# Shift outputs and expert biases moved by DMA instead of TensorE transposes, an early sigmoid table, and a split reciprocal, in a hybrid decoder layer

## The reference, cut to what matters

```python
h = rms_norm(x, norm1) * (1 + sc1) + sh1             # modulation rows from silu(c) @ w_mod
q, k, v, p_rw, g_a, g_b = split(h @ w_in)            # p_rw has RW_COLS = 1792 columns
o_a = sliding_window_attention(q, k, v, cache)       # 8 query heads, 2 key heads
o_b, new_wkv = rwkv7_mix(p_rw, state_shift, state_wkv, ...)
new_shift = p_rw[:, -1]                              # output: last row of p_rw, per sequence
x = x + gt1 * ((sigmoid(g_a)*(o_a@w_pa) + sigmoid(g_b)*(o_b@w_pb)) @ w_o)
h2 = rms_norm(x, norm2) * (1 + sc2) + sh2
# mixture of experts, 32 experts, top 4:
u = h2 @ w1[e] + b1[e]                               # 2048 columns: gate half, linear half
y = (min(u_g,7) * sigmoid(1.702*u_g) * (clip(u_l,-7,7) + 1)) @ w2[e] + b2[e]
```

## Time and profile before

| what | value |
|---|---|
| median of 3 runs | 1269.61 us (1265.81 to 1270.17) |
| profiled execution, its own time | 1269.29 us |
| its span in the profile | 1267.5 us |
| mean granted TensorE clock | 0.992 of full |
| HBM read | 463.91 MB |
| PE, DVE, ACT, POOL busy | 1199.1, 489.7, 266.5, 54.3 us |

### The profile page before, as it was taken

One profiled execution on the slowest core, in us unless ns is written; L12 is line 12 of the kernel. 1 busy time (PEld: TensorE's weight loads), 2 busy tenths in 40 slices (PEclk: granted clock), 3 DMA queues, 4 the chain that ended last, 5 costly groups with the idle time before them and its releaser, 6 DMA issues.

```text
span 1267.5 us, 20297 instructions
## 1 busy us (share of the span) xinstructions
PE 1199.1 (95%) x8057; PEld 576.9 (46%) x8057; DVE 489.7 (39%) x1067; ACT 266.5 (21%) x495; POOL 54.3 (4%) x69
## 2 busy tenths in 40 slices
PE   7999999999999999999999999999999999999998
PEld 5887777788743333333333333333333333333333
DVE  3155756555433334433333333333333333333433
ACT  2013651220321112211112112111111122121110
POOL 0010624000000000000000000000000000000000
PEclk9999999999999999999999999999999999999999
DMA  9976331367699999999999999999999999999996
GB/s 369 381 260 250 110 110 70 102 225 304 248 429 423 415 430 431 430 430 431 432 432 431 432 431 431 431 432 432 431 431 431 431 431 431 432 432 431 430 430 271
DMA packets 57906, 467.22 MB, mean 369 GB/s; under 512 B 5245, under 2 KB 8577, under 8 KB 32618
## 3 DMA queue, kind: packets, MB, share of 16 engines
q1 hardware_dynamic: 55098, 460.55, 86.9%
q0 software_dynamic: 1664, 5.20, 1.5%
q10 hardware_dynamic: 1088, 0.66, 0.2%
HBM read 463.91 MB, written 5.09 MB: 370 GB/s over the span
## 4 chain that ended last, share of the span: by engine, by line
PE 67%; DMA 27%; ACT 2%; DVE 2%; issue 1%; SPq 0%; DVEq 0%
DMA ring<-in_w 27%; PE ps L1557 21%; PE ps L1582 12%; PE ps L972 5%; PE ps L1483 3%; PE ps L962 3%; PE ps L1506 3%; PE ps L1431 2%; PE ps L1399 2%; PE ps L1568 2%; PE ps L980 1%; PE ps L1490 1%; ACT PH L843 1%; PE ps L941 1%; PE ps L917 1%
## 5 line engine op out<-in xcount | busy, mean ns | idle before, releaser
L1557 PE MATMUL ps<-ring,PH 128*64 128x512 f32 x1472 | 327.5, 594 | 23.8 <-DMA ring<-in_w 23.7
L2231 DVE TENSOR_TENSOR SQ<-ps,SQ 128x512 f32<-128x512 f32 x124 | 77.0, 683 | 411.9 <-PE ps L1506 411.8
L1557 PEld LDWEIGHTS ps<-ring,PH 128*64 128x64 f32 x1472 | 103.6, 137 | 239.6 <-issue 188.8
L1582 PE MATMUL ps<-ring,PH 128*64 128x512 f32 x736 | 163.0, 595 | 0.0
L838 ACT COPY PH<-ps 128x512 f32<-128x512 f32 x62 | 33.3, 589 | 576.6 <-PE ps L1557 576.6
L1557 PE MATMUL ps<-arena,PH 128*64 128x512 f32 x504 | 112.2, 594 | 7.5 <-DMA arena<-in_w 7.5
L1582 PEld LDWEIGHTS ps<-ring,PH 128*64 128x64 f32 x736 | 50.8, 137 | 95.8 <-issue 95.8
L1557 PEld LDWEIGHTS ps<-arena,PH 128*64 128x64 f32 x504 | 35.3, 137 | 82.5 <-issue 65.6
L972 PE MATMUL ps<-PH,ring 128*128 128x264 f32 x304 | 69.3, 388 | 0.2 <-issue 0.2
L2224 DVE TENSOR_TENSOR PH<-ps,XR 128x512 f32<-128x512 f32 x31 | 21.4, 692 | 108.4 <-PE ps L1582 108.4
L972 PEld LDWEIGHTS ps<-PH,ring 128*128 128x128 f32 x304 | 57.3, 190 | 10.7 <-issue 1.1
(11 more groups left out here) (485 smaller groups left out, 1173.8 us busy)
## 6 DMA issues: line engine op xcount, KB each, us to landing
ring<-in_w SPq DMA_DIRECT2D x143, 2048.0 KB, 31.5
arena<-in_w SPq DMA_DIRECT2D x46, 2048.0 KB, 31.6
ring<-in_w_mod SPq DMA_DIRECT2D x12, 2048.0 KB, 14.5
ring<-in_w_in SPq DMA_DIRECT2D x8, 2048.0 KB, 12.1
ring<-in_w_o SPq DMA_DIRECT2D x2, 2048.0 KB, 10.7
ring<-in_w_in SPq DMA_DIRECT2D x2, 1024.0 KB, 17.3
ring<-in_w_pa SPq DMA_DIRECT2D x1, 2048.0 KB, 8.1
ring<-in_w_pb SPq DMA_DIRECT2D x1, 2048.0 KB, 9.0
```

Source lines behind the costliest of these rows:

```text
L1557: last = mm(ps[64 * lin:64 * lin + 64, 2 + hh, :], XG[:, k % 4, k // 4, :], slot_row(slot, c, k % 2, lin * FE + hh * 512), start=(k == 0), ...
L1582: last = mm(ps[64 * hh:64 * hh + 64, 4, :], AC[:, f, :], slot_row(slot, c, f % 4, hh * 512), start=(f == 0), stop=(f == NF - 1))
L2231: v.tensor_tensor(acc, ps[:, banks[p // 2][p % 2], :], acc, ALU.add).then_inc(sem["comb_used"], 1)
```

## The change

There are four edits.

1. Shift outputs. The 14 PE transposes and four ACT copies go. POOL copies the nine columns of the 14 chunks into `SHC` (the first 126 floats of `b1T`'s space), and SP, right behind win 6, issues nine DMAs that write `SHC` out element by element: 128 partitions x 14 chunks, each element 4 bytes long in memory order.
2. Expert biases. The load of `b1r`, four PE transposes and a DVE copy go. Behind win 8 SP waits until the nine shift DMAs are done, and loads `b1` straight into `b1T` with features on partitions; `b1T` has its last two dimensions exchanged, so that a piece of 16 bytes is contiguous on both sides.
3. ACT: a one-element sigmoid stands ahead of `mod_rows(8)`, so that the sigmoid table is loaded there.
4. DVE: the reciprocal of the key norms is cut in two halves, the second behind the scans.

```diff
-        b1T = sb("b1T", [P, 4, NE * 4])
+        b1T = sb("b1T", [P, NE * 4, 4])
+        SHC = view(b1T[:, :, :].rearrange("p a b -> p (a b)"), 0, 14, 1 + NS)
@@ SP, the stream
                 if g == AFTER_RWKV[0]:
                     sp.wait_ge(sem["carry_evac"], 5)
-                    sp.wait_ge(sem["sh_out"], 32)
                 if (kind, j) == ("win", 1):
-                    sp.dma_start(b1r, io["b1"].rearrange("(r a) f -> r (a f)", a=4)).then_inc(sem["ld_setup"], 16)
+                if (kind, j) == ("win", 6):
+                    sp.wait_ge(sem["sh_copied"], 1)
+                    for b in range(1 + NS):
+                        row = io["shift_sample"][b - 1:b, :] if b else io["shift_prompt"]
+                        sp.dma_start(row.rearrange("o (c p) -> p c o", p=P), SHC[:, :, b:b + 1],
+                                     allow_slow_non_contiguous=True).then_inc(sem["sh_out"], 16)
+                if (kind, j) == ("win", 8):
+                    sp.wait_ge(sem["sh_out"], 16 + 16 * NS)
+                    sp.dma_start(b1T[:, :, :], io["b1"].rearrange("(r x) y -> r (x y)", x=4).rearrange("r (p f) -> p r f", f=4)).then_inc(sem["ld_b1"], 16)
@@ POOL
-            pool.wait_ge(sem["sh_evac"], 4)
-            pool.dma_start(io["shift_prompt"], ssr[0:1, :]).then_inc(sem["sh_out"], 16)
-            pool.dma_start(io["shift_sample"], ssr[1:9, :]).then_inc(sem["sh_out"], 16)
+            pool.wait_ge(sem["a_evac"], a_end("win4"))
+            pool.tensor_copy(SHC[:, :, :], PTv[:, CR:NCH, NP - 1:T]).then_inc(sem["sh_copied"], 1)
@@ ACT
+            act.activation(warm, epsc[0:1, 0:1], ACT.Sigmoid)
             mod_rows(8)
-            for i in range(4):
-                act.wait_ge(sem["sh_t"], i + 1)
-                w = min(512, RW - 512 * i)
-                act.copy(ssr[0:9, 512 * i:512 * i + w], ps[0:9, 6 + i % 2, 0:w]).then_inc(sem["sh_evac"], 1)
@@ PE
-            for i in range(4):
-                last = tr(ps[:, 7, i * P:i * P + P], b1r[:, i::4], ID)
@@
-            for i in range(4):
-                if i >= 2:
-                    pe.wait_ge(sem["sh_evac"], i - 1)
-                for c in range(4 * i, min(4 * i + 4, 14)):
-                    last = tr(ps[0:9, 6 + i % 2, (c % 4) * P:(c % 4) * P + P], PTv[:, CR + c, NP - 1:T], ID)
-                last.then_inc(sem["sh_t"], 1)
@@ DVE
-            v.tensor_copy(b1T[:, :, :], ps[:, 7, :].rearrange("p (f r) -> p f r", f=4)).then_inc(sem["setup_ready"], 1)
-            chain(v.reciprocal(Rn, Rn))
+            chain(v.reciprocal(Rn[:, 0:2, :], Rn[:, 0:2, :]))
...
             done(v.tensor_tensor(eM, CS, LD[:, :, 0:NP], ALU.subtract), "cs_ready", 2)
+            chain(v.reciprocal(Rn[:, 2:4, :], Rn[:, 2:4, :]))
             chain(v.scalar_tensor_tensor(out=NK, in0=NK, scalar=-1.0, in1=Rn, op0=ALU.mult, op1=ALU.mult))
@@ DVE, before the first expert
+            dve.wait_ge(sem["ld_b1"], 16)
```

More of the change, by code:

```diff
@@ L203, in build @@
         OA = view(PT, 0, 4, T)
-        prow, b1r, ext = view(SG, 2048, P), view(SG, 2176, 512), view(SG, 2688, 384)
+        prow, ext = view(SG, 2048, P), view(SG, 2688, 384)
         crow, csig = view(BM, 0, D), view(BM, 1024, D)
@@ L503, in _ @@
             pool.wait_ge(sem["kmod_ready"], 1)
+            pool.wait_ge(sem["sh_copied"], 1)
             pool.memset(Qz, 0.0).then_inc(sem["pool_part"], 1)
@@ L508, in _ @@
             pool.wait_ge(sem["decays"], 4)
-            pool.wait_ge(sem["sh_t"], 4)
             def by_chunk(x):
@@ L561, in _ @@
             pool.wait_ge(sem["ob_ready"], 1)
-            pool.wait_ge(sem["sh_out"], 32)
+            pool.wait_ge(sem["sh_out"], 16 + 16 * NS)
             pool.wait_ge(sem["st_s"], 32)
@@ L677, in _ @@
             gates(0)
-            act.wait_ge(sem["sh_t"], 4)
+            act.wait_ge(sem["sh_copied"], 1)
             for hp in range(4):
@@ L1011, in _ @@
             pe.wait_ge(sem["ld_cst"], 16)
-            pe.wait_ge(sem["ld_setup"], 48)
-            for i in range(4):
-                last = tr(ps[:, 7, i * P:i * P + P], b1r[:, i::4], ID)
+            pe.wait_ge(sem["ld_setup"], 32)
             for i in range(14):
@@ L1051, in _ @@
             for kv, (t0, nt) in enumerate(TILES[1:]):
-                pe.wait_ge(sem["sh_evac"], 3 + kv)
                 mm(ps[:, 6 + kv, 0:T], II[64 * kv:64 * kv + 64, :], PTv[64 * kv:64 * kv + 64, CK, :], start=True, stop=True)
@@ L1803, in _ @@
             done(last, "setup_ready", 2)
-            dve.wait_ge(sem["ld_setup"], 48)
+            dve.wait_ge(sem["ld_setup"], 32)
             v.tensor_copy(tabx[0:NE, :].rearrange("p (b h) -> p b h", h=HQ), tab[:, :].unsqueeze(1).broadcast_to([NE, NS, HQ])).then_inc(sem["tab_ready"], 1)
             dve.wait_ge(sem["setup_t"], 6)
-            v.tensor_copy(b1T[:, :, :], ps[:, 7, :].rearrange("p (f r) -> p f r", f=4)).then_inc(sem["setup_ready"], 1)
-            chain(v.tensor_copy(SS[:, :, :], ps[:, 5, 0:112].rearrange("p (a b) -> p a b", b=NS)))
+            done(v.tensor_copy(SS[:, :, :], ps[:, 5, 0:112].rearrange("p (a b) -> p a b", b=NS)), "setup_ready", 3)
             v.tensor_copy(brow[:, 0:KEYS], ps[0:NS * HQ, 5, 256:256 + KEYS]).then_inc(sem["brow_ready"], 1)
@@ L1991, in bank @@
                 return ps[:, i, :].rearrange("p (a b) -> p a b", b=CH)
-            dve.wait_ge(sem["sh_out"], 32)
             for n in range(2):
@@ L2241, in hidden @@
                 dve.wait_ge(sem["ut_done"], 2 * i + hh + 1)
-                chain(v.tensor_tensor(UG, u[:, 0], b1T[:, :, column(hh)].broadcast_to([P, 4, C]), ALU.add))
+                chain(v.tensor_tensor(UG, u[:, 0], b1T[:, column(hh), :].rearrange("p r f -> p f r").broadcast_to([P, 4, C]), ALU.add))
                 v.tensor_scalar(UG, UG, 7.0, None, ALU.min).then_inc(sem["ug_ready"], 1)
-                chain(v.tensor_tensor(UL, u[:, 1], b1T[:, :, column(2 + hh)].broadcast_to([P, 4, C]), ALU.add))
+                chain(v.tensor_tensor(UL, u[:, 1], b1T[:, column(2 + hh), :].rearrange("p r f -> p f r").broadcast_to([P, 4, C]), ALU.add))
                 chain(v.tensor_scalar(UL, UL, 7.0, -7.0, ALU.min, ALU.max))
```

## The result

The changed kernel takes 1316.38 us (median of 4, 1314.76 to 1318.56) against 1268.54 us (1265.81 to 1270.17): a ratio of 1.0377, 95% interval 1.0359 to 1.0396. It is slower by 47.8 us, in the direction of rival A and far beyond the range. Its profiled execution took 1315.11 us with a span of 1313.3, which is 45.8 more than before's. Two executions of one later kernel, e8, fell in a slower state of the chip, and ratios leave such executions out.

The account below looks back on a forecast made before the run. The chain of waits before 340 us was taken to set when the DMA-bound expert part starts. Only DVE's 0.9 us gain counted, all else hidden: 1269.6 - 0.9 = 1268.7 us, range 1264 to 1275.

Parts of the forecast that it names:

- rival A: Shift writes ahead of modulation 9: small pieces land late above 31 ns each; at 49.6 ns PE stands 18 us, 1287; chance 0.13.
- The bound: Whole kernel: a microsecond on the chain of waits before 340 us moves the end by one; in the expert loop, nothing.
- PE's path: PE around 120 us: with transposes removed, decay products start at 121.2 instead of 124.27, 3.1 us earlier.
- the cover of the table load: ACT near 118 us: the sigmoid table load of 1.28 us is hidden by modulation 8.
- DVE's side: DVE after the decays: second half reciprocal 3.4 us, normalised keys start at 132.3 instead of 133.19, 0.9 us gained.
- The first probabilities are there at 144.7, PE waits: First group's softmax: DVE and ACT deliver at 144.7; PE, ready at about 142.7, waits 2 us for them.
- rival B: Attention loop: PE's new wait lowers the clock, filler and transposes slow; 1272; chance 0.20.
- the 0.9 us: Gain from normalised keys starting earlier on DVE, the only gain counted in the forecast sum.
- POOL's copy: POOL before the shift writes: 126 elements a partition, done before win 6 is issued at 119.51, costs nothing.
- The price of a piece: DMA cost of one small piece: between 6.6 and 24.8 ns on an engine, taken as 10 ns.
- the 10 us for the shift writes: Nine shift writes behind win 6: 1008 pieces an engine at 10 ns, ending before modulation 9 is delayed, nothing paid.
- Hidden too: Bias load behind win 8: goes in at 197, ends by 222, before pa is issued at 244.22; costs nothing.

Follow-up runs that it names:

- e8: e7 with the reciprocal of the key norms whole again, ahead of the scans; 1271.12 us against 1268.95, ratio 1.0003.
- e9: Kernel before with only the early one-element sigmoid and the reciprocal cut in halves; 1269.4 us against 1268.95, ratio 0.9997.
- e1: Changed kernel with shift rows written in 1,152 pieces of 56 bytes in place of 16,128 of 4; 1272.85 us against 1269.29, ratio 1.0033.
- e2: Kernel of only SP's DMAs, each pattern alone, without the layer; 4-byte writes as in the change 58 ns a piece, reads of that shape 14.
- e5: Changed kernel with shift columns turned by one PE transpose and written in 126 pieces of 512 bytes; 1273.64 us against 1269.29, ratio 1.0028.
- e7: e5 with the bias load moved from behind win 8 to behind win 6; 1267.24 us against 1268.95, ratio 0.9984.
- e4: Changed kernel with the 4-byte shift writes moved behind win 8 and the bias load behind wo 1; 1308.58 us against 1269.29, ratio 1.0313.
- e13: e7 with four filler steps moved ahead of the second scores and POOL's query memset started earlier; 1267.14 us against 1268.88, ratio 0.9979.

## Why the prediction was wrong, by its own steps

- **The bound, PE's path and the cover of the table load: right.** The large delay ahead of 340 us came out at the end one for one (45.3 us at the first expert's load, 45.8 at the end of the span); for a delay of 1.2 us the rule did not hold in e9, where it was gone by pa. The table load is hidden, the products start at 121.34 (121.2 forecast) at a clock of 1.00.
- **DVE's side: right in its steps.** Second half of the reciprocal 3.45 us (3.4), keys at 132.56, and 132.09 in e1 (132.3). PE's wait for DVE was 3.4 us where 2 were forecast, and it came ahead of the second scores, for the copy of the queries, not behind the filler.
- **"The first probabilities are there at 144.7, PE waits": the first half right, the second wrong, because rival B came true as well.** They were there at 144.97. But the filler behind PE's wait took 6.2 to 6.5 us where 3.83 is the full clock's time, and the first transposes came at 146.5 to 147.1, behind before's 145.79. The granted clock of 140 to 150 us was 0.69 in the changed kernel, 0.74 in e1, 1.00 before. That ate the 0.9 us and some 0.7 to 1.3 more. B, given 0.20, had the mechanism right; its price for all groups together was 2.3 us above before, and at the first group 0.7 to 1.3 were seen.
- **POOL's copy: right**, 0.28 us at 115.90, hidden.
- **"The price of a piece": the step that failed.** Its two bounds, 6.6 and 24.8 ns, were both drawn from reads of HBM into SBUF of 512 bytes and more, and applied to writes of 4 bytes to HBM. The reads of e2 lie within them (11 to 14 ns); the writes measured 58 ns alone and some 73 in the kernel. So the term of the sum that failed is the 10 us for the shift writes, with the nothing that was to be paid for them. Rival A had the mechanism, the place and the threshold (31 ns) right, and was worth 18 us at the price it was given. At the price measured alone, 58 ns, its own sum gives 133 + 58 + 7.7 - 172.3 = 26 us, where PE waited 37.8 and the issue behind modulation 9 came 40.9 late. The 73 us close that gap, but they are read back from the landing of modulation 9 and so confirm nothing. In the gap the engines also carried POOL's state load, for which A had no term; how much of it that load explains, no run shows. The size of A's terms and its chance, 0.13, were off. The Trainium skill's rule ("DMA: Bandwidth & Descriptors", Specifications: below 512 bytes a read-modify-write) spoke for it. The runs agree in that writes of 4 and 16 bytes are dear, but place the edge lower, between 16 and 64 bytes: 64-byte writes cost 13 ns, and 4-byte reads 14, neither with a penalty to be seen. Whether a read-modify-write is what costs, no run shows.
- **"Hidden too", of the bias load: wrong, 3 to 6 us.** As a transfer it was hidden, and its 17 us are within the 25 allowed. What it held up, as far as the traces tell, were PE's instruction fetches on the same engines. Shown: moving that one load (e5 to e7) turns 4.3 us above before into 1.7 below, 6.1 us in all, and brings PE's waits back to before's size. That instruction fetches are the link is inferred: from waits in the middle of a series without semaphores, from blocks that take 0.93 us without small pieces, 1.4 beside 16-byte reads, 4.2 beside 4-byte writes, and from long stalls that each begin with or during such a slow block and end 1.2 to 4.4 us behind it. The prediction had no term for this: it asked only whether a weight block or PE's data would be late.

Open stay the spread of e8, what makes up the 15 ns between 58 and 73, why the writes in e4 (50 ns) are cheaper than alone (58), and why modulation 9's pieces were still slow after the last small write had gone.

## What to carry to other kernels

Price a transfer by a row of the same direction, size and place in memory, or measure it alone: a bound from reads said nothing of 4-byte writes to HBM here. Replacing PE transposes by element-wise DMA trades idle or hidden microseconds for time of a queue that everything behind it shares; one transpose of all 126 columns moves them out in pieces of 512 bytes, and with the bias load behind win 6 that kernel is the faster one (0.9984; with the bias load behind win 8 it is at 1.0028). In this kernel the transfer of many small pieces belonged where PE ran large matmuls, not beside hundreds of small ones: late for no weight block, it still held up PE.

## What the runs showed of the hardware that was not expected

- Writes to HBM of 4 bytes, as in the change, and of 16 bytes side by side cost 58 ns a piece on an engine, and 4-byte writes 102 where one partition writes words side by side; 64-byte writes cost 13 ns, less than 512-byte writes (30) and less than a 4-byte write in 512 bytes of its own (30).
- SP did not run ahead of slow pieces: the nine DMAs of 7 KB held its issue for 68.44 us as writes, and for 21.15 as reads.
- Instruction blocks of 16 KB move over the same engines as data, and one that took about 1 us took up to 6.1 beside 4-byte writes (e4). PE stood up to 8.4 us at a time there, in the middle of a series of equal matmuls.
- The clock adds to a small loss: after a wait of 3.4 us 16 products took 6.46 us where 3.83 is usual, and after stalls of 2.5 and 2.7 us 62 matmuls took 1.71 us where 0.93 is usual. After a wait of 0.7 us (e13) the granted clock of the 10 us around was 1.00.
